# Reordering adjacent seven-product units and moving a weight difference to Pool

## The reference

```python
hn = rms_norm(h, norm_ffn_g[layer])
h = h + (jax.nn.silu(hn @ ffn_w_gate[layer]) * (hn @ ffn_w_up[layer])) @ ffn_w_down[layer]
```

## Time and profile before

| | |
|---|---|
| median of 3 runs | 565.21 us (565.13 to 565.22) |
| the profiled execution | 565.53 us |
| its span, first to last instruction | 563.4 us |
| TensorE's granted clock, mean | 0.997 |
| busy: TensorE, its weight loads | 553.5 us (98%), 469.1 us (83%) |
| busy: VectorE, ScalarE, Pool | 480.2 us (85%), 340.9 us (61%), 14.9 us (3%) |
| read from HBM | 104.1 MB |

### The profile page before, as it was taken

One profiled execution on the slowest core, in us unless ns is written; L12 is line 12 of the kernel. 1 busy time (PEld: TensorE's weight loads), 2 busy tenths in 40 slices (PEclk: granted clock), 3 DMA queues, 4 the chain that ended last, 5 costly groups with the idle time before them and its releaser, 6 DMA issues.

```text
span 563.4 us, 7508 instructions
## 1 busy us (share of the span) xinstructions
PE 553.5 (98%) x2877; PEld 469.1 (83%) x2877; DVE 480.2 (85%) x568; ACT 340.9 (61%) x471; POOL 14.9 (3%) x54
## 2 busy tenths in 40 slices
PE   9999999999999999999999999999999999999996
PEld 8899988888888888778888888888888888887785
DVE  5769996789997999996797998977799889999955
ACT  5877664756664773764566356546477548567524
POOL 1200001000000000000000000000000000000000
PEclk9999999999999999999999999999999999999998
DMA  8995444461378046276469522434706850734401
GB/s 288 410 401 197 184 149 149 151 225 76 135 275 337 1 190 258 112 282 243 151 250 346 186 74 76 167 138 171 271 1 225 311 212 10 283 156 151 186 1 74
DMA packets 30563, 105.65 MB, mean 188 GB/s; under 512 B 3392, under 2 KB 4544, under 8 KB 30528
## 3 DMA queue, kind: packets, MB, share of 16 engines
q1 hardware_dynamic: 30384, 105.04, 49.9%
q10 hardware_dynamic: 144, 0.14, 0.1%
HBM read 104.11 MB, written 1.05 MB: 187 GB/s over the span
## 4 chain that ended last, share of the span: by engine, by line
PE 84%; DVE 14%; ACT 1%; issue 1%; DVEq 0%; ACTq 0%
PE bank L1773 18%; PE bank L1775 18%; PE bank L1774 18%; DVE w_lo L1084 8%; PE bank L2218 8%; PE bank L2221 4%; PE bank L1884 4%; DVE raw L1646 3%; PE bank L1887 2%; PE bank L1834 1%; PE bank L1837 1%; PE bank L1830 1%; PE bank L1856 1%; DVE work L1654 1%; PE bank L1976 1%; PE bank L1769 1%
## 5 line engine op out<-in xcount | busy, mean ns | idle before, releaser
L1084 DVE TENSOR_TENSOR w_lo<-raw,w_hi 128x2048 fp32r<-128x2048 f32 (+2 forms) x98 | 217.3, 2229 | 13.4 <-ACT w_hi L614 13.3
L614 ACT ACTIVATE w_hi<-raw 128x2048 fp32r<-128x2048 f32 (+2 forms) x81 | 149.3, 1859 | 6.9 <-PE bank L1775 3.6
L1773 PE MATMUL bank<-w_lo,yT_hi 128*128 128x512 f32 (+1 forms) x242 | 96.2, 397 | 1.9 <-DVE w_lo L1084 1.9
L1775 PE MATMUL bank<-w_hi,yT_lo 128*128 128x512 f32 (+1 forms) x242 | 94.0, 389 | 0.0
L1774 PE MATMUL bank<-w_hi,yT_hi 128*128 128x512 f32 (+1 forms) x242 | 93.9, 388 | 0.0
L1773 PE MATMUL bank<-w_lo,xT 128*128 128x512 f32 (+1 forms) x184 | 71.5, 389 | 0.0
L1775 PE MATMUL bank<-w_hi,xT 128*128 128x512 f32 (+1 forms) x184 | 70.3, 382 | 0.0
L1774 PE MATMUL bank<-w_hi,xT 128*128 128x512 f32 (+1 forms) x184 | 70.0, 380 | 0.0
L931 ACT ACTIVATE w_hi<-raw 128x2048 fp32r<-128x2048 f32 x24 | 45.9, 1913 | 16.7 <-DVE raw L1646 16.7
L1773 PEld LDWEIGHTS bank<-w_lo,yT_hi 128*128 128x128 f32 x242 | 45.5, 188 | 11.2 <-issue 2.7
L1775 PEld LDWEIGHTS bank<-w_hi,yT_lo 128*128 128x128 f32 x242 | 45.4, 188 | 9.7
(11 more groups left out here) (240 smaller groups left out, 881.3 us busy)
## 6 DMA issues: line engine op xcount, KB each, us to landing
raw<-in_slabs SPq DMA_DIRECT2D x170, 512.0 KB, 4.6
spare<-in_slabs SPq DMA_DIRECT2D x16, 512.0 KB, 4.2
raw<-in_slabs SPq DMA_DIRECT2D x5, 256.0 KB, 5.3
h<-in_x SPq DMA_DIRECT2D x2, 512.0 KB, 6.4
early<-in_norm_ffn_g SPq DMA_DIRECT2D x2, 512.0 KB, 10.0
raw<-in_slabs SPq DMA_DIRECT2D x6, 128.0 KB, 4.8
h<-in_x_cols SPq DMA_DIRECT2D x1, 512.0 KB, 5.9
early<-in_norm_mix_g SPq DMA_DIRECT2D x1, 512.0 KB, 8.1
```

The costliest lines, as they stand in the source:

```text
L614: A(w_hi[:, s % SLOTS, c], raw_of(r, c), ACT.Copy).then_inc(hi_ready, 1)
L1084: V.tensor_tensor(w_lo[:, s % SLOTS, c], raw_of(preps[s][0], c), w_hi[:, s % SLOTS, c].bitcast(F32), ALU.subtract).then_inc(lo_ready, 1)
L1773: T.matmul(o, st_hi, mv_lo, start=first, stop=False, skip_group_check=onto)
L1775: return T.matmul(o, st_lo, mv_hi, start=False, stop=last, skip_group_check=onto)
```

## The change

Three things are changed. In each unit the third difference (y = z - x) is made by Pool in place of VectorE: layer 0's three are queued behind the power of the norm ahead of that layer's feed forward stage, and layer 1's behind the same of layer 1. Pool waits for t3's low part and the second sum; `block_sum` counts as before, and VectorE's fourth difference now waits for the third, Pool's. The first difference of unit 6 moves ahead of unit 3's last low part of activations.

VectorE's and ScalarE's orders change: in all units the low part of the slab behind t4 moves ahead of the first sum, or the sum moves ahead of t4's low part (unit 8); in unit 8 the gates, turned activations and low parts are interleaved anew, and on ScalarE the second copy moves from behind b22's high part to ahead of t1's. Unit 6's last gate moves behind t3's low part.

On TensorE the turn of unit 6's j = 3 moves from the middle of b11 to the middle of t3 (and to bank 5), and the third turn of each unit from ahead of the down product to between its two blocks of columns; the waits for low parts of activations that stood there are gone or come with the product.

```diff
--- before.py
+++ after.py
@@ -458,9 +458,9 @@
 
             return len(TURNED) * (l + 1) + 4 * seven_no(l, i) + j + 1
 
-        def turned(j):
-
-            return bank[:, (7, 5, 7, 6)[j], 0:256]
+        def turned(l, a, j):
+
+            return bank[:, (7, 5, 7, 5 if a + 2 in SEVEN_AT[l] else 6)[j], 0:256]
 
         def sum_no(l, n):
 
@@ -589,6 +589,13 @@
                     step(nc.gpsimd.memset(per_count[r, g // 2, t:t + 1], 1.0 / (t + 1)))
             assert made[0] == CONSTS_MADE
 
+            def third_difference(l, a):
+
+                x, y, z, _ = (raw_of(r) for r, _ in place["raw", l, a])
+                pool.wait_ge(lo_ready, place["t3", l, a] + 1)
+                pool.wait_ge(block_sum, 4 * seven_no(l, a) + 2)
+                nc.gpsimd.tensor_tensor(y, z, x, ALU.subtract).then_inc(block_sum, 1)
+
             for n, (kind, a, b) in enumerate(POWS):
                 pool.wait_ge(pow_asked, n + 1)
                 if kind == "norm":
@@ -598,6 +605,9 @@
                 else:
                     o, i, e = rstd[:, 2:4], meansq[:, 2:4], power[:, 0:2]
                 nc.gpsimd.tensor_tensor(o, i, e, ALU.pow).then_inc(pow_done, 1)
+                if (kind, a, b) in (("norm", 1, 1), ("norm", 3, 1)):
+                    for unit in SEVEN_AT[a // 2]:
+                        third_difference(a // 2, unit)
 
 
         @block.scalar
@@ -935,7 +945,7 @@
 
                 def chunk(i, p):
 
-                    next_hi(2)
+                    next_hi(1 if i + 1 in SEVEN_AT[l] and in_seven(l, i - 1) else 2)
                     if i == 2:
                         forms_split()
                     pair_low(i, 0)
@@ -978,7 +988,7 @@
 
                     act.wait_ge(act_t, seven_turn_no(l, a, j))
                     half, ip = SEVEN_HALF[j], half_of_acts(l, a + SEVEN_CHUNK[j])
-                    A(actT_hi[:, half, 2 * ip:2 * ip + 2, :].rearrange("p k t -> p (k t)"), turned(j),
+                    A(actT_hi[:, half, 2 * ip:2 * ip + 2, :].rearrange("p k t -> p (k t)"), turned(l, a, j),
                       ACT.Copy).then_inc(at_hi, 1)
 
                 def seven(a):
@@ -986,14 +996,28 @@
                     if a - 2 in SEVEN_AT[l]:
                         next_hi()
                         seven_copy(a, 0)
-                        next_hi(3)
+                        seven_hi(a - 2, 3)
+                        seven_copy(a, 1)
+                        next_hi(4)
+                        seven_copy(a, 2)
+                        seven_silu(a, 0)
+                        next_hi(2)
+                        seven_silu(a, 1)
+                        seven_hi(a, 0)
+                        seven_silu(a, 2)
+                        seven_hi(a, 1)
+                        seven_hi(a, 2)
+                        seven_silu(a, 3)
+                        next_hi(2)
+                        seven_hi(a, 3)
+                        return
                     else:
                         seven_copy(a, 0)
                         next_hi(2)
-                    seven_copy(a, 1)
-                    next_hi(3)
-                    seven_copy(a, 2)
-                    seven_silu(a, 0)
+                        seven_copy(a, 1)
+                        next_hi(3)
+                        seven_copy(a, 2)
+                        seven_silu(a, 0)
                     if a + 2 not in SEVEN_AT[l]:
                         next_hi()
                     seven_silu(a, 1)
@@ -1005,7 +1029,10 @@
                         next_hi()
                     seven_silu(a, 3)
                     next_hi()
-                    seven_hi(a, 3)
+                    if a + 3 in SEVEN_AT[l]:
+                        next_hi()
+                    if a + 2 not in SEVEN_AT[l]:
+                        seven_hi(a, 3)
 
                 for i in range(2, NCH - 1):
                     if i in SEVEN_AT[l]:
@@ -1611,13 +1638,13 @@
 
                 def chunk_before_seven(i, p, a):
 
-                    block_add(a, 0)
+                    if i == 2 or not in_seven(l, i - 1):
+                        block_add(a, 0)
                     next_lo()
                     block_add(a, 1)
                     pair_sum(i, 0)
                     next_lo()
                     swiglu(2 * i, 0)
-                    block_add(a, 2)
                     act_lo(2 * i, 0, p)
                     if i == 2:
                         split_forms()
@@ -1639,7 +1666,7 @@
                         dve.wait_ge(raw_loaded[r], made)
                     if m:
                         dve.wait_ge(lo_ready, place[("b11", "t3", "t2")[m - 1], l, a] + 1)
-                    if m in (1, 2):
+                    if m in (1, 3):
                         dve.wait_ge(block_sum, 4 * seven_no(l, a) + m)
                     x, y, z, e = (raw_of(r) for r, _ in raws)
                     o, p, q = ((y, z, y), (x, y, x), (y, z, x), (x, e, x))[m]
@@ -1666,41 +1693,67 @@
                     dve.wait_ge(at_hi, U + 2 * a + j + 1)
                     half, ip = SEVEN_HALF[j], half_of_acts(l, a + SEVEN_CHUNK[j])
                     hi, lo = (t[:, half, 2 * ip:2 * ip + 2, :].rearrange("p k t -> p (k t)") for t in (actT_hi, actT_lo))
-                    V.tensor_tensor(lo, turned(j), hi.bitcast(F32), ALU.subtract).then_inc(at_lo, 1)
+                    V.tensor_tensor(lo, turned(l, a, j), hi.bitcast(F32), ALU.subtract).then_inc(at_lo, 1)
 
                 def seven(a):
 
-                    b = a + 2 if a + 2 in SEVEN_AT[l] else None
+                    follows, leads = a - 2 in SEVEN_AT[l], a + 2 in SEVEN_AT[l]
+                    next_lo()
+                    if follows:
+                        next_lo()
+                        block_add(a, 3)
+                    else:
+                        next_lo()
+                        block_add(a, 3)
                     next_lo(2)
-                    block_add(a, 3)
-                    next_lo(3)
-                    seven_add(a, 0)
-                    next_lo()
-                    seven_gate(a, 0)
-                    next_lo()
+                    if follows:
+                        seven_add(a, 0)
+                        next_lo()
+                        seven_gate(a, 0)
+                        next_lo()
+                        seven_add(a, 1)
+                        seven_gate(a, 1)
+                        seven_act_lo(a, 0)
+                        seven_gate(a, 2)
+                        seven_act_lo(a, 1)
+                        next_lo()
+                        seven_add(a, 2)
+                        seven_act_lo(a, 2)
+                        seven_gate(a, 3)
+                        next_lo()
+                        if not ends_mixed(l, a):
+                            next_lo()
+                        seven_act_lo(a, 3)
+                        return
+                    else:
+                        next_lo(2)
+                        seven_add(a, 0)
+                        next_lo()
+                        seven_gate(a, 0)
                     seven_add(a, 1)
                     seven_gate(a, 1)
                     seven_gate(a, 2)
                     seven_act_lo(a, 0)
-                    if b:
-                        block_add(b, 0)
+                    if leads:
+                        block_add(a + 2, 0)
                     seven_act_lo(a, 1)
                     seven_act_lo(a, 2)
-                    if b:
-                        block_add(b, 1)
+                    if leads:
+                        block_add(a + 2, 1)
                     seven_add(a, 2)
-                    if b:
+                    if leads:
+                        next_lo()
                         seven_gate(a, 3)
                         next_lo()
                         seven_act_lo(a, 3)
+                        return
+                    next_lo()
+                    seven_gate(a, 3)
+                    if not ends_mixed(l, a):
                         next_lo()
-                        block_add(b, 2)
-                    else:
-                        next_lo()
-                        seven_gate(a, 3)
-                        if not ends_mixed(l, a):
-                            next_lo()
-                        seven_act_lo(a, 3)
+                    if a + 3 in SEVEN_AT[l]:
+                        block_add(a + 3, 0)
+                    seven_act_lo(a, 3)
 
                 for i in range(2, NCH - 1):
                     if i in SEVEN_AT[l]:
@@ -2225,7 +2278,7 @@
 
                     pe.wait_ge(act_ready, U + 2 * a + j + 1)
                     for k in range(2):
-                        last = T.transpose(turned(j)[:, k * P:(k + 1) * P], seven_out[j][:, k * P:(k + 1) * P],
+                        last = T.transpose(turned(l, a, j)[:, k * P:(k + 1) * P], seven_out[j][:, k * P:(k + 1) * P],
                                            ident[:, :])
                     last.then_inc(act_t, 1)
 
@@ -2278,9 +2331,8 @@
                         pe.wait_ge(summed, sum_no(l, 2 * a - 1))
```

(9 more changed lines are left out.)

## The result

The changed kernel takes 574.44 us (median of 4 runs, 573.83 to 576.34) against 565.17 us (564.93 to 565.22) for the kernel before, run beside it: a ratio of 1.017, 95% interval 1.0145 to 1.0196. It is **slower by 9.3 us**. The forecast was 569.1 us, the range ended at 572.0; the side was right, the size was not. The profiled execution took 573.86 us with a span of 572.0 us.

A forecast was written before the change was run, and what follows sets the result against it. TensorE bounds the kernel, VectorE the second of two adjacent units. Units 8, 3 and 6 add 0.9 + 1.0 + 0.1 = 2.0 per layer, twice: +3.9 on 565.21 gives 569.1 us; range 563.3 to 572.0.

The forecast's parts named there:

- The hold: While Pool's third difference reads SBUF, no VectorE instruction with two SBUF inputs can start, for the whole 4.6 us.
- rival 2: Half speed: VectorE and Pool both progress, VectorE at half rate while Pool reads; +0.8 per layer, 566.9 us; chance 0.13.
- rival 3: Pool first: in unit 8 Pool enters ahead of the gate at 226.1; +7.8 in all, 573.0 us; chance 0.12.
- First wait in unit 8: In rival 3, t2's low part is done only at 233.4, where TensorE wants it at 230.1: +3.4.
- The ScalarE chain: Unit 8: ScalarE's copy, t1's high and low parts, fourth difference and b21's low part make b21 late: +1.3.
- Units 3 and 6: VectorE, held by Pool there, makes TensorE late: +1.0 in unit 3, +0.15 in unit 6, per layer.
- +0.4 at the second down product: Unit 8: the second gate's low part comes after the third gate, so the second down product starts some 0.4 late.
- Pool's time: A third difference on Pool takes 4.6 us, estimated from memset and copy rows; ends 2.3 and 6.3 us.
- Costed at nothing: TensorE's moved turn, ScalarE's reordered copies, SyncE's loads, Pool's powers and VectorE's fourth difference waiting for Pool add no time.
- rival 1: No hold: Pool works unnoticed, unit 8's first wait vanishes, b21 comes late; -0.8 per layer, 563.6 us; chance 0.32.

The follow-up runs named there:

- x2: Changed kernel with Pool's third difference replaced by a memset that reads nothing, the subtraction left out: 563.01 us, ratio 0.9965.
- x8: Changed kernel with Pool copying one block in place of the difference, the subtraction left out: 564.52 us, ratio 0.9988.
- x3: Changed kernel, but in unit 8 Pool also waits for t2's low part, so it enters behind that instruction: 569.76 us, ratio 1.0092.
- x7: Changed kernel with each Pool difference cut into four instructions of 512 columns, the last of which counts: 573.96 us, ratio 1.0156.
- x9: Kernel before, with only the third differences moved to Pool and the engines' old orders kept: 576.17 us, ratio 1.0198.
- x4: All differences on VectorE in the new order, with three VectorE steps around unit 8 moved: 560.52 us, ratio 0.992 against the kernel before.
- x5: Changed kernel, but Pool makes only unit 8's third differences and VectorE those of units 3 and 6: 573.27 us, ratio 1.0134.

## Why the prediction was wrong in its size

- **The hold: right.** Given somewhat better than even odds (0.55) from rows that all showed something else, it is there and exclusive. The rule of the Trainium skill (SBUF — State Buffer, Who interferes with whom) agrees with the runs: only against a GpSimd instruction that reads (2.29 us beside the memset of x2, 3.98 beside the copy of x8), only for two SBUF inputs (0.42 us with one in PSUM in x3, 4.28 with both in SBUF in the change), a whole instruction at a time (x7). Half speed (rival 2) is excluded: the held low part ends 2.15 us after Pool.
- **The step that failed** is the sentence "Back to back VectorE instructions start 2.20 us apart and last 2.28, so they leave no gap; I take it that Pool gets in at VectorE's next pause". Pool got in as soon as its conditions held, during the gate and ahead of t2's low part, which is rival 3, to which I gave 0.12. x7 shows the rule behind it: one that waits gets its turn as soon as the instruction that runs ends, also between back-to-back ones. x3, with the pause enforced, gives 569.76. So this step is worth 574.44 - 569.76 = 4.7 us, the whole miss but 0.7. Both medians have some slow clock in them; the fastest runs of the two, 573.83 and 568.9, are 4.9 us apart.
- **Rival 3's terms.** First wait in unit 8: +3.4 against TensorE's due time, measured 3.37 and 3.39. The ScalarE chain: 1.3, measured 1.11 and 1.22. Units 3 and 6: +1.0 and +0.15 by my working, measured 0.93 and 0.13 at the next units' starts. Its +0.4 at the second down product did not come: there is no wait there. And its 573.0 lacks what no sum had, the next point.
- **The clock, not priced.** 1.4 us in the profiled execution, in one layer; more or less in other executions, so that four runs spread over 2.5 us (573.83 to 576.34), and four of the kernel before over 0.3.
- **Pool's time: right by luck.** Estimated 4.6 us from the earlier trace rows; measured 4.58 and 4.59 alone (x9, x3), 4.71 to 4.75 in the change, where Pool, by this difference, first waits some 0.15 us for the VectorE instruction that runs. Its two parts were each off by over 1 us, and cancelled (see the last section). The Trainium skill (GPSIMD Engine Reference, Performance versus the Vector engine) has 4497 ns for an addition of this size, 2% below what this case shows for the subtraction.
- **The chances.** Slower at 0.55 was the right side but too weak, and 0.12 on "Pool first" had no row behind it: the conditions of Pool were seen to hold at 226.2 while its start was put at 228.8, on a guess about who wins.
- **Costed at nothing: right** so far as the rows go: the waits of TensorE that are new or longer all end with VectorE, none with a load or a power.
- **Slips in the sums.** The forecast's own terms make 4.0 to 4.1 us, where it has 3.9 (twice 0.9 + 1.0 + 0.1 or 0.15); rival 1's 242.4 - 241.2 is 1.2, where it has 1.3; rival 2's terms make 0.7, where it has 0.8. Nothing hangs on them.

Open: why the clock fell after a wait of 3.2 to 3.7 us in some executions and layers and not in others. x9 has a wait of 3.69 us with eight slow starts behind it in layer 0, and one of 3.70 with none in layer 1. Nothing was tried that sets the length of such a wait alone.

## What to carry to other kernels

Before moving work from VectorE to Pool, see what both read. A Pool instruction that reads SBUF stops VectorE's instructions with two SBUF operands for its full length, so the exchange was 4.7 us against 2.3, and it hits whatever is issued first after Pool's conditions hold. Make Pool wait for the instruction that must not be late (x3 won 4.7 us by that, and was still 4.8 us slower than the kernel before), or give Pool work that only writes. And look at the length of TensorE's longest wait: the waits of unit 8 behind which the clock fell were of 3.2 to 3.7 us, and x7, with the loss in waits of at most 1.5 us, kept the full clock. What the move was meant to buy, an earlier low part, was to be had by order alone (x4: -4.5 us).

## What the runs showed that I had not expected

- A VectorE instruction with one operand in PSUM and one in SBUF is not held (0.42 us beside a 4.59 us Pool instruction, x3); one of the same shape with both in SBUF is (4.28 us, the change).
- A held instruction shows as a long duration, 6.69 instead of 2.28 us, not as idle time ahead of it, on VectorE and on Pool alike (3.34 us for a quarter of which 1.15 was work).
- On Pool 128x2048 float32 take 1.81 us to set, 2.04 us to copy and 4.71 us to subtract, the last two at the same place of unit 8, where both start within a VectorE instruction: the second tensor, with the subtraction, costs 2.7 us. By the earlier trace rows I had put it at 1.4 us (0.69 ns x 2048) and the copy at 3.2 (1.53 ns x 2048 and 93 ns): two errors of about 1.2 us that cancelled.
- Waits of 3.2 to 3.7 us of TensorE were followed, in some executions, by matmuls 0.43 us apart (seven in the change's layer 0), the 1.2 GHz level. In the change's profiled execution the first matmuls after the wait still ran 0.23 us apart; the slow ones began 1.3 us later. In x3 and x5 the first matmul after it already took 0.57 us to the next start.
